# TensorE's moving operands: rows of 1,280 bytes that begin at one offset modulo 256

## The reference

```python
# first block
h = modulate(rmsnorm(x, norm1_g), shift1, scale1)
qa, ka, va, qb, kb, vb, ga, gb = split(h @ w_in)
merged = sigmoid(ga) * (swa(qa, ka, va) @ w_branch_a) + sigmoid(gb) * (moba(qb, kb, vb) @ w_branch_b)
x = x + gate1 * (merged @ w_out)
h2 = modulate(rmsnorm(x, norm2_g), shift2, scale2)
x = rmsnorm(x + gate2 * (square(relu(h2 @ w_mlp_in)) @ w_mlp_out), final_g)
# second block, two layers, on 16 meta tokens + 256 tokens
h = concat([meta, x])
for l in range(2):
    h = h + 0.5 * swiglu(rmsnorm(h), gate_up_down of ffn1[l])      # 1024 -> 2816 -> 1024
    u = rmsnorm(h, mix_norm[l])
    h = h + (pool_mixer(u) if l == 0 else mla_attention(u, shared k, v))
    h = h + 0.5 * swiglu(rmsnorm(h), gate_up_down of ffn2[l])
    if l == 0: shared k, v = up-projections of rmsnorm(h, kv_in_norm) @ w_dkv
out = rmsnorm(h, final_norm)[16:]
```

## Time and profile before

| | us |
|---|---|
| median of three runs | 1,235.67 |
| lowest and highest | 1,234.13 and 1,235.68 |
| the profiled execution's own time | 1,234.03 |
| its span, first to last instruction | 1,232.3 |
| TensorE busy in it | 1,208.6 |
| VectorE busy in it | 862.2 |

### The profile page before, as it was taken

One profiled execution on the slowest core, in us unless ns is written; L12 is line 12 of the kernel. 1 busy time (PEld: TensorE's weight loads), 2 busy tenths in 40 slices (PEclk: granted clock), 3 DMA queues, 4 the chain that ended last, 5 costly groups with the idle time before them and its releaser, 6 DMA issues.

```text
span 1232.3 us, 23766 instructions
## 1 busy us (share of the span) xinstructions
PE 1208.6 (98%) x9956; PEld 1185.4 (96%) x9956; DVE 862.2 (70%) x1214; ACT 633.9 (51%) x985; POOL 172.2 (14%) x178
## 2 busy tenths in 40 slices
PE   6999999999999999999999999999999999999997
PEld 4999999999999999999999999999999988999996
DVE  6789888776756766556766656766666777766654
ACT  6557546675545444434544444454444567544541
POOL 3024323000322000012200001320001221000021
PEclk9999999999999999999999999999999999999999
DMA  9997775667564555654455565456556533555551
GB/s 361 321 338 269 240 251 172 240 235 261 168 220 154 177 172 172 204 173 136 124 185 171 172 204 173 148 180 201 177 191 200 188 120 95 203 199 177 191 164 35
DMA packets 67563, 239.17 MB, mean 194 GB/s; under 512 B 7380, under 2 KB 9573, under 8 KB 67456
## 3 DMA queue, kind: packets, MB, share of 16 engines
q1 hardware_dynamic: 66800, 235.41, 57.2%
q0 software_dynamic: 656, 2.24, 0.5%
HBM read 236.55 MB, written 1.07 MB: 193 GB/s over the span
## 4 chain that ended last, share of the span: by engine, by line
PE 93%; DVE 2%; issue 0%; ACT 0%; POOL 0%; DVEq 0%
PE G L611 28%; PE G L610 28%; PE G L612 28%; PE A L610 1%; PE A L612 1%; PE A L611 1%; DVE sb_wlo L1568 0%; PE A L762 0%; PE A L1056 0%; PE A L777 0%; PE A L750 0%; PE G L1111 0%; PE G L1112 0%; PE G L1113 0%; PE A L1090 0%; PE A L640 0%
## 5 line engine op out<-in xcount | busy, mean ns | idle before, releaser
L1568 DVE TENSOR_TENSOR sb_wlo<-sb_raw,sb_whi 128x1024 fp32r<-128x1024 f32 (+1 forms) x398 | 487.9, 1258 | 77.4 <-ACT sb_whi L1169 77.3
L610 PE MATMUL G<-sb_xh,sb_whi 128*128 128x256 f32 (+2 forms) x1752 | 496.5, 283 | 0.4 <-DVE sb_wlo L1568 0.4
L611 PE MATMUL G<-sb_xl,sb_whi 128*128 128x256 f32 (+2 forms) x1752 | 496.8, 284 | 0.0
L612 PE MATMUL G<-sb_xh,sb_wlo 128*128 128x256 f32 (+2 forms) x1752 | 495.1, 283 | 0.0
L1169 ACT ACTIVATE sb_whi<-sb_raw 128x1024 fp32r<-128x1024 f32 (+1 forms) x397 | 404.5, 1045 | 175.5 <-PE G L612 156.9
L610 PEld LDWEIGHTS G<-sb_xh,sb_whi 128*128 128x128 f32 x1752 | 329.7, 188 | 0.9 <-DVE sb_wlo L1568 0.7
L612 PEld LDWEIGHTS G<-sb_xh,sb_wlo 128*128 128x128 f32 x1752 | 329.3, 188 | 0.0
L611 PEld LDWEIGHTS G<-sb_xl,sb_whi 128*128 128x128 f32 x1752 | 329.2, 188 | 0.0
L610 PE MATMUL G<-sb_hh,sb_whi 128*128 128x256 f32 (+1 forms) x1056 | 296.0, 280 | 1.5 <-DVE sb_hh L1809 1.4
L612 PE MATMUL G<-sb_hh,sb_wlo 128*128 128x256 f32 (+1 forms) x1056 | 296.1, 280 | 0.0
L611 PE MATMUL G<-sb_hl,sb_whi 128*128 128x256 f32 (+1 forms) x992 | 279.0, 281 | 0.0
(11 more groups left out here) (335 smaller groups left out, 1225.2 us busy)
## 6 DMA issues: line engine op xcount, KB each, us to landing
sb_raw<-in_wstream SPq DMA_DIRECT2D x438, 512.0 KB, 4.4
sb_raw<-in_wstream SPq DMA_DIRECT2D x8, 320.0 KB, 7.6
sb_bias<-bias_scratch POOLq DMA_DIRECT2D x1, 2048.0 KB, 16.8
sb_X<-in_xT SPq DMA_DIRECT2D x2, 512.0 KB, 5.1
out_T<-sb_X SPq DMA_DIRECT2D x4, 256.0 KB, 2.7
sb_con<-in_consts SPq DMA_DIRECT2D x1, 601.0 KB, 10.1
sb_band<-in_bands SPq DMA_DIRECT2D x1, 314.0 KB, 5.1
sb_vec<-in_vecs SPq DMA_DIRECT2D x1, 82.5 KB, 2.0
```

Source lines behind the costliest of these rows:

```text
L610: e.matmul(out, w_h, xs, start=k0 + s.kt == 0, stop=False)
L611: e.matmul(out, w_h, xr, start=False, stop=False)
L612: m = e.matmul(out, w_l, xs, start=False, stop=k0 + s.kt == ktotal - 1)
L1568: e.tensor_tensor(wlo[:, i % NSPLIT, 0:w], raw[:, c % NRAW, 0:w], f(whi[:, i % NSPLIT, 0:w]), ALU.subtract).then_inc(lo_done, 1)
```

## The change

- `xh`, `xl` get rows of `ROW` = 320 values, 1,280 bytes or five times 256. The 32-value buffer `pad` goes ahead of them and moves `xh` from 128 to 0 modulo 256, `xl` too. `sq` moves up behind `xl`, which keeps `whi` and `wlo` at 128. The other small buffers are put in another order, and `hh`, `hl` and what overlays them stay at 64.
- What a dense stage reads from `xh`/`xl` starts at column 16, 64 bytes into the row: `COLS1` as before; `ALL` is now written and read at columns 16 to 287 (`wide`) for `ffn1_0`, the pool mixer and `ffn2_0`; `SHIFT` is now columns 16 to 273, with the two shift columns behind the tokens. `ffn1_1`'s input stays at column 0 and is read from column 16.
- Hidden rows of the 272-column stages in `hh`/`hl` are 320 apart (`hid_cols`), and so are `kvcols`. Only 3 of the 8 rows of the key-value input fit behind the hidden ones; rows 3 to 7 go to new buffers `kin_h`, `kin_l`, which overlay `oh` and `ol`.
- `mean_ones` loses columns (its third part has 56 instead of 128, of which one is read), to make room; `latents` moves behind `cqh`, `cql`.
- `band` overlays `oh` as well. Its load moves from `wout0` to `mlp_in4`, behind a wait of SyncE for the last matmul of `brb3`.

```diff
+ROW = 320
+KIN = 3
-        xh, xl = sb("xh", [P, KT, T], F32R), sb("xl", [P, KT, T], F32R)
+        sb("pad", [P, 32])
+        xh, xl = sb("xh", [P, KT, ROW], F32R), sb("xl", [P, KT, ROW], F32R)
+        sq = sb("sq", [P, 2, T])
...
-        mean_ones = sb("mean_ones", [P, 3, P])
+        mean_ones = sb("mean_ones", [P, 2 * P + 56])
...
+        with ExitStack() as s:
+            band = sb("band", [P, BANDC], to=s)
+        with ExitStack() as s:
+            kin_h, kin_l = sb("kin_h", [P, KT - KIN, ROW], F32R, to=s), sb("kin_l", [P, KT - KIN, ROW], F32R, to=s)
         oh, ol = sb("oh", [P, 8, SEQ], F32R), sb("ol", [P, 8, SEQ], F32R)
-        kvx = FF2 * T
+        kvx = FF2 * ROW
...
-        SHIFT = slice(META - 2, T)
+        SHIFT = slice(META, T + 2)
+        wide = lambda cols: slice(cols.start + META, cols.stop + META)
-        kvcols = lambda kt: slice(kvx + kt * T, kvx + (kt + 1) * T)
+        kvcols = lambda kt: slice(kvx + kt * ROW, kvx + kt * ROW + T)
+        kv_high = lambda kt: hh[:, kvcols(kt)] if kt < KIN else kin_h[:, kt - KIN, ALL]
-        sh_cols = lambda t: t[:, :, META - 2:META]
+        sh_cols = lambda t: t[:, :, T:T + 2]
+        hid_cols = lambda f_, j: slice(j * ROW, j * ROW + T) if FFN_COLS[f_] == ALL else slice(j * SEQ, (j + 1) * SEQ)
...
-                if c == where["wout0"][0][0]:
+                if c == where["mlp_in4"][0][0]:
+                    e.wait_ge(mm_done, ended["brb3"])
                     e.dma_start(band[:, :], bands).then_inc(band_in, 16)
...
-                src = lambda kt: (xh[:, kt, cols], xl[:, kt, cols])
+                at = wide(ALL) if cols == ALL else cols
+                src = lambda kt: (xh[:, kt, at], xl[:, kt, at])
...
-                hid = lambda kt: (hh[:, kt * n:(kt + 1) * n], hl[:, kt * n:(kt + 1) * n])
+                hid = lambda kt: (hh[:, hid_cols(f_, kt)], hl[:, hid_cols(f_, kt)])
...
-                e.tensor_copy(shift_out[:, b, :], g[:, :, 0])
+                e.tensor_copy(shift_out[:, b, :], g[:, :, SEQ])
-                e.tensor_tensor(hf(i), g[:, :, 2:2 + SEQ], rb, ALU.mult).then_inc(left_dve, 1)
+                e.tensor_tensor(hf(i), g[:, :, 0:SEQ], rb, ALU.mult).then_inc(left_dve, 1)
```

More of the change, by code:

```diff
@@ L511, in build_program @@
         COLS1, ALL = slice(META, T), slice(0, T)
-        SHIFT = slice(META - 2, T)
+        ones_of = lambda which: mean_ones[:, which * P:min((which + 1) * P, 2 * P + 56)]
+        SHIFT = slice(META, T + 2)
+        wide = lambda cols: slice(cols.start + META, cols.stop + META)
         REV = lambda ap: ap[:, :, ::-1]
@@ L639, in mean @@
                 for k, part in enumerate(parts):
-                    m = e.matmul(A[bank][:, 0:n], mean_ones[:, which, :], part, start=k == 0, stop=k == len(parts) - 1)
+                    m = e.matmul(A[bank][:, 0:n], ones_of(which), part, start=k == 0, stop=k == len(parts) - 1)
                 m.then_inc(mean_done, 1)
@@ L905, in mix @@
                     for out, a, m in zip(outs, (META, META + P, 0), (P, P, META)):
-                        x_h, x_l = xh[:, 2 * gi + kt, a:a + m], xl[:, 2 * gi + kt, a:a + m]
+                        x_h, x_l = (x[:, 2 * gi + kt, wide(slice(a, a + m))] for x in (xh, xl))
                         opens = gi % 2 == 0 and kt == 0
@@ L919, in token_means @@
                 for n, a in enumerate((META, META + P, 0)):
-                    m = e.matmul(A[0][:, n:n + 1], sumsq[:, a:a + P], mean_ones[:, 0, 0:1], start=True, stop=True)
+                    m = e.matmul(A[0][:, n:n + 1], sumsq[:, a:a + P], ones_of(0)[:, 0:1], start=True, stop=True)
                 m.then_inc(mean_done, 1)
@@ L1012, in query_means @@
                     cols = slice(META + n * P, META + (n + 1) * P)
-                    m = e.matmul(A[0][:, n:n + 1], sumsq[:, cols], mean_ones[:, 0, 0:1], start=True, stop=True)
+                    m = e.matmul(A[0][:, n:n + 1], sumsq[:, cols], ones_of(0)[:, 0:1], start=True, stop=True)
                 m.then_inc(mean_done, 1)
@@ L1016, in query_means @@
                     for kt in range(QR):
-                        m = e.matmul(A[1][:, n:n + 1], cqf[:, kt, n * P:(n + 1) * P], mean_ones[:, 2, 0:1], start=kt == 0, stop=kt == QR - 1)
+                        m = e.matmul(A[1][:, n:n + 1], cqf[:, kt, n * P:(n + 1) * P], ones_of(2)[:, 0:1], start=kt == 0, stop=kt == QR - 1)
                 m.then_inc(mean_done, 1)
@@ L1150, in tensor_program @@
             e.wait_ge(sumsq_done, SUMSQ["ffn2_1"] - 1)
-            e.matmul(out, mean_ones[:, 0, :], sumsq[:, COLS1], start=True, stop=False)
+            e.matmul(out, ones_of(0), sumsq[:, COLS1], start=True, stop=False)
             e.wait_ge(sumsq_done, SUMSQ["ffn2_1"])
-            e.matmul(out, mean_ones[:, 0, :], sq[:, LAST_SQ, COLS1], start=False, stop=False)
+            e.matmul(out, ones_of(0), sq[:, LAST_SQ, COLS1], start=False, stop=False)
             e.wait_ge(last_square, 1)
-            e.matmul(out, mean_ones[:, 0, :], sq[:, 1 - LAST_SQ, COLS1], start=False, stop=True).then_inc(mean_done, 1)
+            e.matmul(out, ones_of(0), sq[:, 1 - LAST_SQ, COLS1], start=False, stop=True).then_inc(mean_done, 1)
         def scalar_program(e):
@@ L1183, in sqrt_mean, with x_hi @@
                 e.activation(root[:, cols], A[bank][:, 0:cols.stop - cols.start], ACT.Sqrt, bias=eps_c[:, 0:1]).then_inc(root_done, 1)
-            def x_hi(name, i, cols, gain, after=None):
+            def x_hi(name, i, cols, gain, after=None, at=None):
                 for t in range(2):
@@ L1189, in x_hi @@
                     e.wait_ge(left_dve, plan.left_dve[f"{name}{i}"] - 1 + t)
-                    e.activation(xh[:, kt, cols], X[:, kt, cols], ACT.Identity, scale=gain(kt)).then_inc(xh_done, 1)
+                    e.activation(xh[:, kt, at or cols], X[:, kt, cols], ACT.Identity, scale=gain(kt)).then_inc(xh_done, 1)
                     if after:
@@ L1386, in scalar_program @@
                     e.wait_ge(meta_scaled, 1)
[L1387 to L1388 removed]
+                    e.activation(xh[:, :, wide(slice(0, META))], scaled_m, ACT.Copy).then_inc(meta_hi, 1)
+                x_hi("mlp_out", i, COLS1, lambda kt: g1m[:, kt:kt + 1], square_final, at=wide(COLS1))
             def swiglu(f_, factor, hooks, between=None, late=False):
@@ L1625, in residual, with x_lo @@
                                            ALU.mult, ALU.add).then_inc(left_dve, 1)
-            def x_lo(stage, i, cols, gain):
+            def x_lo(stage, i, cols, gain, at=None):
+                at = at or cols
                 for t in range(2):
```

39 lines of the change are left out of this document (19 added, 20 removed).

## The result

The kernel is not faster. The changed one takes 1,236.57 us (median of 20 runs, 1,235.11 to 1,237.49), the one before 1,234.62 (20 runs, 1,233.39 to 1,235.68). The ratio is 1.0016, with a 95% interval of 1.001 to 1.0022. I had forecast 1,218.8, so 17.8 us are missing, and the range is missed too. The profiled execution took 1,235.3 us (span 1,233.6).

What follows compares the result with a forecast made beforehand. TensorE, busy 98% of the span, was taken as the bound, its rate read from matmul start spacing. Terms 7.6 + 5.5 + 2.8 + 0.7 + 0.3 = 16.9 us off 1,235.7 gave 1,218.8 us, range 1,212 to 1,228.

Steps and rivals of the forecast that it cites:

- step 1: Gate and up of ffn1_1 and ffn2_1: 2,112 matmuls of 256 columns from 116.9 to 113.3 ns, 7.6 us less.
- the near bound, -1.9 us: Gate and up of ffn1_1 and ffn2_1: loss of 1.9 us if their matmuls run at the slow 117.8 ns.
- The rival "long streams lock": Long streams at 64 stay slow: 4.7 us per gate-and-up stream; one or two locked, 1,221 to 1,229 us, chance 0.25.
- Step 6: 256-column stages on hh (wout, mlp_out, second layer's down), about 2,000 matmuls: unchanged at 113.3 ns.
- Step 3: mlp_in: 768 matmuls of 258 columns from 119.5 to 115.8 ns, 2.8 us less, bounds 1.5 and 4.1.
- Step 2: All 3,264 matmuls of 272 columns: from 125.0 to 123.3 ns, 5.5 us less.
- The far bound of 120.0 ns: 272-column matmuls reaching 120.0 ns: 16.3 us less; better than 123.3 ns had chance 0.08.
- Step 4: Gates between the first attention's scores, 384 matmuls: 0.7 us less, bounds 0 and 1.4.
- Step 5: dq0 and dq1: 72 matmuls by 3.6 ns, 0.3 us less; stage qk and the v stage behind it, nothing.
- Step 7: band's later load, behind a wait for brb3's end: costs nothing, as the wait is 34 us old when reached.
- Step 8: ScalarE and VectorE write the same element counts; VectorE stays under 72% in gate and up; no engine replaces TensorE.

Runs made afterwards that it cites:

- experiment 8: Changed kernel with weights starting at 0 instead of 128 modulo 256, and 272-column matmuls starting mlp_out0, ffn1_1_gu2 and ffn2_1_gu2: 1,248.29 us, ratio 1.0107.
- experiment 11: Changed kernel with weights at 160, hh/hl at 96, mean_ones at 32, mlp_in at 192 modulo 256, and 272-column matmuls starting five stretches: 1,233.83 us, ratio 0.9996.
- experiment 4: Changed kernel with xh/xl back at their old rows and columns; hidden and key-value rows stay 320 apart: 1,232.49 us, ratio 0.9983.
- Experiment 1: Changed kernel with the first three matmuls of ffn1_1_gu2 and of ffn2_1_gu2 made 272 columns wide (a kick): 1,223.39 us, ratio 0.991.
- experiment 5: Changed kernel with mlp_in's operand at 192 modulo 256 and 272-column matmuls starting mlp_out0, ffn1_1_gu2 and ffn2_1_gu2: 1,221.38 us, ratio 0.9903.
- experiment 6: Changed kernel with mlp_in's operand at 0 modulo 256 and 272-column matmuls starting mlp_out0, ffn1_1_gu2 and ffn2_1_gu2: 1,223.78 us, ratio 0.9908.
- experiment 7: Changed kernel with mlp_in's operand at 128 modulo 256 and 272-column matmuls starting mlp_out0, ffn1_1_gu2 and ffn2_1_gu2: 1,223.62 us, ratio 0.9905.
- experiment 9: Changed kernel with mlp_in at 192 modulo 256 and 272-column matmuls starting wout1, mlp_out1, mlp_out3, ffn1_1_gu2, gu11, gu15 and ffn2_1_gu2: 1,225.12 us, ratio 0.9926.
- experiment 2: Changed kernel with only the first three matmuls of ffn1_1_gu11 made 272 columns wide: 1,231.6 us, ratio 0.9973.
- experiment 3: Changed kernel with row 7 of xh/xl starting 48 values later in ffn1_1 and ffn2_1, at 0 modulo 256: 1,224.85 us, ratio 0.9922.
- experiment 10: Changed kernel with the mean issued nine matmuls later in ffn1_1 and three later in ffn2_1, no wide matmul: 1,236.63 us, ratio 1.0015.
- experiment 12: Changed kernel with mean_ones declared ahead of con, at 32 instead of 0 modulo 256, no wide matmul: 1,227.93 us, ratio 0.9935.

## Why the prediction was wrong

- **Mechanism of step 1: right in part, and the step that failed.** The place of the operands does set the spacing (experiments 8 and 11). What I read off was that offset 64 *allows* 113.3 ns; what I put in the sum was that the streams *take* it. The earlier trace rows had shown the other rhythm, and I held it for an exception of short pieces. Both long streams took the slow one behind the mean, and the near bound, -1.9 us, was the case (-1.7 measured). The rival "long streams lock" had this mechanism and its 4.7 us a stream, with a chance of 0.25; I had priced it for gate and up alone.
- **Step 6, "unchanged at 113.3", failed for the same reason.** A down stage follows its gate and up without a gap, and inherits the rhythm: 2 x 528 matmuls by 4.45 ns, 4.7 us, measured +2.0 and +2.3. (In `ffn1_1` the quick down stage meets a wait of 0.2 us for `sb_wlo`, which the slow one doesn't.) Before, with rows of `xh` at four offsets, both down stages started quick. I take it that the old mixture of offsets protected the down stages; no run isolates that, but in experiment 4, with the old rows of `xh`, they are quick as before. `wout` was drawn slow as well (+0.7), `mlp_out` was not.
- **Step 3 was mis-sized, in sign too.** 258 columns at 64 pay 13.3 ns, not 8.3: 120.8 ns. Instead of -2.8 us, +1.0; no offset tried gives under 118.6. I had interpolated between 256 and 272 columns, which have better rows.
- **Step 2 was right to the digit.** 123.3 ns, from the six matmuls of the earlier trace rows; -5.2 us with all that stands between these stages, where 5.5 was forecast. The far bound of 120.0 ns never showed.
- **Step 4 held roughly**: 1.3 us by `brb3`'s end, where the gates were to give 0.7 and at most 1.4. **Step 5 didn't**: `dq0`, `dq1` inherited 117.8 ns, and the stage has +0.1 us. **Step 7 held**: `band` is issued at 191.6 us, when the last matmul of `brb3` is 25 us old. **Step 8 held**: VectorE 861.7 us, TensorE 98%, no new releaser in the window above.

The sum again, from the 1,234.62 that the kernel before has over 20 runs: less 16.9, plus 9.4 for two slow gate-and-up streams, 4.7 for the down stages behind them, 3.8 for `mlp_in` (768 x 5.0 ns) and 0.7 for `wout` is 1,236.3 us; measured were 1,236.57. Experiment 1 is the check on the largest items: with the two streams and their down stages quick the time is 13.2 us less, where the account has 9.4 + 4.7, and 0.7 for `wout`, which was quick there, less the 1.7 us (383 x 4.45 ns) that `mlp_out0` and `mlp_out1` lost: 13.1.

Open is what in the mean's addresses decides, and whether the rhythm is drawn or determined. For determined: behind the mean 18 of 18 slow; all twelve kicks of slow `xh` streams (both `gu2` in experiments 1, 5, 6, 7 and 9, `gu11` in 2, `gu15` in 9) led to quick; all five kicks of quick streams (`gu11` in 9, `wout1` and `mlp_out3` in 9 and 11) led to slow. Against: of the nine kicks of `hh` streams (`mlp_out0` in 5 to 7, three each in 9 and 11) one led to quick, `mlp_out0` in 6, and `mlp_out1` stayed slow in 9 and 11. Without a kick, `mlp_out0` is quick in the changed kernel and in experiment 3 and slow in 1, 2 and 10, though up to there these five kernels have the same instructions at the same addresses: nothing that the program does ahead of it decides that stream's rhythm. And there are the fourth executions of experiments 5 and 12, without a trace. Distances other than the six below were not tried in a whole stream.

## What to carry to other kernels

Where two starts of matmuls lie a few per cent further apart than the best stream's, look at the offsets of *both* operands modulo 256, and judge by starts, never by recorded durations or busy shares, which hardly move (98% in all these kernels). A row that shows a good rhythm shows that it can occur, not that a stream will hold it: price the long streams at both, and carry the state over each border without a gap. And making everything uniform takes away the small disturbances that can pull a stream out of a bad state (experiment 3: one row in eight at another offset, 11.7 us); a change that removes variety needs a reason why the state that is left will be the good one.

## What the runs showed of the hardware

- The same stream of 128x128 by 256-column `float32r` matmuls has two stable rhythms, 113.3 and 117.8 ns, at a granted clock of 1.00. It keeps one over nearly 1,500 matmuls, over borders of stages too. In these traces it changed at a foreign matmul (a float32 one, one of another width, or a row at another offset), and once at a wait of 0.2 us for `sb_wlo`: `ffn1_1`'s down stage in experiment 11, 113.3 ns ahead of it and 117.8 behind. In the kernel before and in eight others the same wait left the stream quick. The page "TensorE: Matmul & The Clock Gate" of the Trainium skill, section "Back-to-back issue gap", has 262 cycles in its table for 256 columns, 109.2 ns, and gives that for a matmul by itself; for a stream of weight loads and matmuls it has figures at 128 and 512 columns only. No run here came under 113.3.
- Spacing by the distance of the moving operand's start above its weights', modulo 256: at 192, 113.3 or 117.8 ns (256 columns), 123.3 (272), 120.8 (258); at 64, 117.8, 126.7 and 118.7 to 119.1; at 160, 117.3 or 118.6 (256) and 123.3 (272). 258 columns take 120.0 to 120.8 at 0, 120.0 at 32, and 120.0 to 122.2 at 128.
- Weight loads and moving operands don't read independently. The Trainium skill's page "SBUF — State Buffer", section "A bandwidth-pool intuition that's wrong (but worth ruling out)", gives the loads a port of their own; moving the weights by 128 bytes, with small buffers that no dense matmul reads, cost 24.9 us here (experiment 8 against 1). That a collision of these two reads is the mechanism is my reading of it; the runs show only that the distance counts.
